# Second attention of a two-block layer: value products that give their output by channels, shares ahead of the transposes, and the output gate by channels

## The reference, cut to what matters

```python
s = jnp.einsum('bhqd,bhkd->bhqk', qblk, kt).astype(jnp.float32) * scale
p = jax.nn.softmax(s, axis=-1).astype(vt.dtype)
return jnp.einsum('bhqk,bhkd->bqhd', p, vt)
...
attn = dense_bidirectional_attention(q, k, v_a)
u_attn = (attn * jax.nn.silu(z_attn)) @ w_attn_out[l]
gates = jax.nn.sigmoid(jnp.concatenate([gate_hy, gate_attn], axis=-1) + b_gate[l])
merged = g_hy * u_hy + g_at * u_attn
x = x + merged @ w_out[l]
```

## Time and profile before

| | |
|---|---|
| median of 3 runs | 801.56 us (801.39 to 801.56) |
| span of the profiled execution | 802.3 us |
| TensorE products busy | 742.8 us, 93% |
| VectorE busy | 465.3 us, 58% |
| ScalarE busy | 321.6 us, 40% |

### The profile page before, as it was taken

How to read it: one execution, slowest core, us unless ns; L and a number is a source line. 1 busy time by engine, 2 the same in 40 slices (tenths; PEclk the granted TensorE clock), 3 DMA queues, 4 the chain that set the end, 5 groups by cost and what they waited for, 6 DMA issues and landing times.

```text
span 802.3 us, 11034 instructions
## 1 busy us (share of the span) xinstructions
PE 742.8 (93%) x4636; PEld 561.2 (70%) x4636; DVE 465.3 (58%) x825; ACT 321.6 (40%) x479; POOL 17.9 (2%) x15
## 2 busy tenths in 40 slices
PE   7999999999999999996799798689999999989998
PEld 7978876888877886553346254247999966668886
DVE  6878965555756666532243221138687798855673
ACT  6464436537437325210111010037665524245631
POOL 0000000000000000000000000001100003000000
PEclk9999999999999999998779999999999999999999
DMA  9855542233439759899999999995563744433311
GB/s 318 246 189 181 168 158 97 102 106 114 149 94 410 282 208 422 323 363 420 420 421 406 420 421 421 418 398 205 164 213 125 233 144 133 157 105 105 105 52 53
DMA packets 63153, 189.97 MB, mean 237 GB/s; under 512 B 7481, under 2 KB 11835, under 8 KB 51132
## 3 DMA queue, kind: packets, MB, share of 16 engines
q1 hardware_dynamic: 61326, 184.44, 62.1%
q10 hardware_dynamic: 1774, 4.79, 1.8%
HBM read 188.16 MB, written 1.05 MB: 236 GB/s over the span
## 4 chain that ended last, share of the span: by engine, by line
PE 60%; DVE 16%; DMA 15%; ACT 6%; issue 1%; POOL 0%; SPq 0%; ACTq 0%; DVEq 0%
PE pb L519 56%; DMA raw<-in_w_exp_up 6%; DVE rawo L1785 4%; PE pb L528 4%; DMA arena<-in_w_exp_gate 3%; DMA WHo<-in_w_exp_up 3%; ACT WH L1282 2%; DMA WHo<-in_w_exp_down 2%; DVE cv_ L1892 1%; ACT arena L1441 1%; DVE arena L2053 1%; DVE arena L1838 1%; DMA c<-in_cst 0%; POOL small L2687 0%; DVE arena L2099 0%
## 5 line engine op out<-in xcount | busy, mean ns | idle before, releaser
L1785 DVE TENSOR_TENSOR rawo<-raw,WH 128x2048 fp32r<-128x2048 f32 (+5 forms) x80 | 172.7, 2176 | 71.2 <-ACT WH L1282 71.1
L519 PE MATMUL pb<-WH,HTh 128*128 128x512 f32 (+2 forms) x384 | 156.2, 407 | 5.9 <-DVE arena L1838 3.1
L1282 ACT ACTIVATE WH<-raw 128x2048 fp32r<-128x2048 f32 (+5 forms) x80 | 144.0, 1823 | 20.6 <-PE pb L519 15.2
L519 PE MATMUL pb<-rawo,HTh 128*128 128x512 f32 (+2 forms) x384 | 148.8, 387 | 0.0
L519 PE MATMUL pb<-WH,HTl 128*128 128x512 f32 (+2 forms) x384 | 148.6, 387 | 0.0
L519 PEld LDWEIGHTS pb<-WH,HTh 128*128 128x128 f32 x384 | 73.1, 190 | 24.9 <-issue 5.3
L519 PEld LDWEIGHTS pb<-rawo,HTh 128*128 128x128 f32 x384 | 72.8, 190 | 14.6
L519 PEld LDWEIGHTS pb<-WH,HTl 128*128 128x128 f32 x384 | 73.1, 190 | 13.3 <-issue 1.0
L519 PE MATMUL pb<-WH,arenao 128*128 128x512 f32 x192 | 59.6, 392 | 1.2 <-DVE arenao L1819 1.2
L519 PE MATMUL pb<-arena 128*32 128x256 f32 (+6 forms) x252 | 58.4, 433 | 1.8 <-ACT arena L1698 0.7
L519 PE MATMUL pb<-raw,arena 128*32 128x256 f32 (+1 forms) x256 | 49.0, 475 | 10.7 <-DMA raw<-in_w_exp_up 6.1
(11 more groups left out here) (363 smaller groups left out, 1270.5 us busy)
## 6 DMA issues: line engine op xcount, KB each, us to landing
raw<-in_w_in SPq DMA_DIRECT2D x46, 1024.0 KB, 5.1
raw<-in_w_exp_up SPq DMA_DIRECT2D x18, 1024.0 KB, 21.3
arena<-in_w_exp_gate SPq DMA_DIRECT2D x13, 1024.0 KB, 22.5
arena<-in_w_exp_down SPq DMA_DIRECT2D x12, 1024.0 KB, 17.0
WHo<-in_w_exp_down SPq DMA_DIRECT2D x9, 1024.0 KB, 23.2
raw<-in_w_out SPq DMA_DIRECT2D x8, 1024.0 KB, 5.8
raw<-in_w_exp_gate SPq DMA_DIRECT2D x8, 1024.0 KB, 15.9
WHo<-in_w_exp_up SPq DMA_DIRECT2D x8, 1024.0 KB, 22.0
```

The source lines that it names most:

```text
L519: return e.matmul(o, l, r, start=start, stop=stop, skip_group_check=True)
L1282: e.activation(h_, r_, ACT.Copy).then_inc(hi.sem, hi.mark(k))
L1785: e.tensor_tensor(l_, r_, h_.bitcast(F32), ALU.subtract).then_inc(lo.sem, lo.mark(k))
```

## The change

1. The value gate `za` is computed with channels on the partitions (`channel_chunk`: per chunk, four blocks of 128 channels, three products of 256 columns each, two blocks in one bank). VectorE drains it, multiplied by the row `RB` that holds each token's norm; then ScalarE takes Silu in one instruction over all 1024 elements of `ZAT`.
2. VectorE takes the reciprocal of a head's sums and scales its exponentials (`shares2`) at the start of the round; the transposes wait for that (`sn2`) and are written ordered by key block, so that a head's 256 queries stand side by side.
3. Value products take the values as the stationary side (64 columns) and the turned shares as 256 moving columns. Two heads share a bank, one on partitions 0 to 63, one on 64 to 127; they are issued once for two heads, in rounds 4, 6, 8 and 10, in bank 4 or 5 in turn.
4. The output comes out by channels, so the transposes of the output go. VectorE multiplies each pair by the gate (`output_gated`), ScalarE makes the upper half (`output_high`) and VectorE the lower (`output_low`), spread over the rounds.
5. `gate 2` goes to banks 4 and 5; `gate 3`, `branch 0` and `branch 1` stay in 6 and 7.
6. The rows of `w_attn_out` are loaded in the order "(c p)" in place of "(p c)"; `OT2` and `RB` are in other places of the SBUF.

```diff
         RD = arena[:, 6144:6400].rearrange("p (t l) -> p t l", t=2)
-        RB = arena[:, 8192:8448]
+        RB = C["matt"][:, 0:256]
         XNs = [x.bitcast(F32) for x in (XNh, XNl)]
...
         UT = tuple(x[:, 0:1024].rearrange("p (c l) -> p c l", c=4) for x in HD_)
-        OT2 = tuple(x[:, 0:4, :] for x in HT)
+        OT2 = tuple(arena_r[:, o:o + 1024].rearrange("p (c l) -> p c l", c=4) for o in (8704, 9728))
         G1 = arena[:, C1:C1 + 2048].rearrange("p (t d) -> p t d", t=2)
...
         G_ = (G1, G2)
-        ZA = rt_[:, 0:1024].rearrange("p (t d) -> p t d", t=2)
-        O2 = rt_[:, 1024:2048].rearrange("p (t d) -> p t d", t=2)
+        ZAT, OG = (rt_[:, o:o + 1024].rearrange("p (c l) -> p c l", c=4) for o in (0, 1024))
         cqj = [sg_[:, 0:384], sg_[:, 384:768]]
...
             weight(("gate", i), w2, 8, 3232 + 512 * i, 512, "(c p)")
-        for key, w, kc, rows_ in (("whn", whn, 4, "(p c)"), ("wa2", wa2, 4, "(p c)"), ("wo2", wo2, 8, "(c p)")):
+        for key, w, kc, rows_ in (("whn", whn, 4, "(p c)"), ("wa2", wa2, 4, "(c p)"), ("wo2", wo2, 8, "(c p)")):
             for i in range(2):
...
         filler("zh", "zh", HT, "ng", ac, True)
-        filler("za", "za", HT, "ng", ac)
+        filler("za", "za", HT, "ng", ve)
         for i in range(4):
...
 
+            def channel_chunk(name, key, c, o, lhs, ready):
+                k, j, last = chunk_at[key][c]
+                lo.wait_ge(e, k)
+                ve.wait_ge(e, (ready, c))
+                w = tuple(x[:, j, :] for x in tile_parts(k))
+                end = c == len(chunk_at[key]) - 1
+                for i in range(4):
+                    ins = mul3(o[i // 2][:, 256 * (i % 2):256 * (i % 2) + 256], tuple(x[:, 128 * i:128 * i + 128] for x in w),
+                               tuple(x[:, c, :] for x in lhs), c == 0 and i % 2 == 0, end)
+                if last:
+                    ins.then_inc(mm.sem, mm.mark(("tile", k), *([(name, 0), (name, 1)] if end else [])))
+
             def fill(n):
...
                         fill_at.rotate(1)
-                    gemm_chunk(name, key, c, open_fill[name], lhs, ready, turned)
+                    if name == "za":
+                        channel_chunk(name, key, c, open_fill[name], lhs, ready)
+                    else:
+                        gemm_chunk(name, key, c, open_fill[name], lhs, ready, turned)
 
...
             fill_at.clear()
-            fill_at.append(6)
-            held_o2 = [ring.take(("o2", t), ve, at=4 + t) for t in range(2)]
+            fill_at.extend((4, 6, 6, 6))
 
...
                 o = ring.take(("p2", h), (ve, ac)[h % 2])
-                ac.wait_ge(e, ("s2", h))
-                for i in range(4):
-                    ins = turn(o[:, i * 128:i * 128 + 128], S2[:, h % 4, i * 128:i * 128 + 128])
+                ve.wait_ge(e, ("sn2", h))
+                for kk in range(2):
+                    for t in range(2):
+                        ins = turn(o[:, kk * 256 + t * 128:kk * 256 + t * 128 + 128],
+                                   S2[:, h % 4, t * 256 + kk * 128:t * 256 + kk * 128 + 128])
                 ins.then_inc(mm.sem, mm.mark(("p2", h)))
 
-            def values2(h):
-                (ve, ac)[h % 2].wait_ge(e, ("p2", h))
+            def values2(p):
+                o = ring.take(("o2", p), ve, at=4 + p % 2)
+                for h in (2 * p, 2 * p + 1):
+                    (ve, ac)[h % 2].wait_ge(e, ("p2", h))
                 ve.wait_ge(e, (("kv", 1), 0))
                 ac.wait_ge(e, (("kv", 1), 1))
-                for t in range(2):
-                    for kk in range(2):
-                        ins = mul(held_o2[t][:, h * 64:h * 64 + 64],
-                                  P2[h % 4][:, t * 256 + kk * 128:t * 256 + kk * 128 + 128],
-                                  V2[:, kk, h * 64:h * 64 + 64], kk == 0, kk == 1)
-                ins.then_inc(mm.sem, mm.mark(("pv2", h)))
+                for kk in range(2):
+                    for i in range(2):
+                        h = 2 * p + i
+                        ins = mul(o[64 * i:64 * i + 64, 0:256], V2[:, kk, h * 64:h * 64 + 64],
+                                  P2[h % 4][:, kk * 256:kk * 256 + 256], kk == 0, kk == 1)
+                ins.then_inc(mm.sem, mm.mark(("pv2", p)))
 
...
                     weights2_T(h - 2)
-                if h >= 3:
-                    values2(h - 3)
-            fill(2)
-            ve.wait_ge(e, "o2")
-            transposed("o2T", lambda t: O2[:, t, :], 4)
+                if h >= 4 and h % 2 == 0:
+                    values2(h // 2 - 2)
             fill(99)
...
                 elif name == "za":
-                    drain(name, ZA, ACT.Silu, by=rg)
+                    ve.wait_ge(e, ("za", 1))
+                    e.activation(ZAT, ZAT, ACT.Silu).then_inc(ac.sem, ac.mark("zas"))
                 elif name[0] == "gate" and i < 2:
...
 
+            def output_high(p):
+                ve.wait_ge(e, ("og", p))
+                e.activation(OT2[0][:, p, :], OG[:, p, :], ACT.Copy).then_inc(ac.sem, ac.mark(("o2h", p)))
+
             for h in range(11):
...
                     fill(1)
+                if h in (5, 7, 9):
+                    output_high((h - 5) // 2)
                 if 2 <= h <= 9 and h % 2:
                     if h >= 6:
-                        mm.wait_ge(e, ("pv2", h - 6))
+                        mm.wait_ge(e, ("pv2", (h - 6) // 2))
                     drain_t(("p2", h - 2), P2[(h - 2) % 4])
-            for i in (2, 3):
-                sigmoid(i)
-            high("o2T", OT2, 4, after=(("gate", 3), 1))
+            sigmoid(2)
+            output_high(3)
+            sigmoid(3)
             fill(99)
...
                                                op0=ALU.mult, op1=ALU.add).then_inc(ve.sem, ve.mark((name, t)))
+                elif name == "za":
+                    for t in range(2):
+                        mm.wait_ge(e, (name, t))
+                        e.tensor_tensor(ZAT[:, 2 * t:2 * t + 2, :], pb((name, t))[:, :].rearrange("p (c l) -> p c l", c=2),
+                                        RB.unsqueeze(1).to_broadcast([128, 2, 256]), ALU.mult).then_inc(
+                            ve.sem, ve.mark((name, t)))
                 elif name[0] == "branch":
...
 
+            def shares2(h):
+                s = h % 4
+                ac.wait_ge(e, ("s2", h))
+                e.reciprocal(rsum[:, :, h:h + 1], ssum[:, :, h:h + 1]).then_inc(ve.sem, ve.mark(("rs2", h)))
+                ve.wait_ge(e, ("rs2", h))
+                for t in range(2):
+                    cut = S2[:, s, t * 256:t * 256 + 256]
+                    ins = e.tensor_scalar(cut, cut, rsum[:, t, h:h + 1], None, ALU.mult)
+                ins.then_inc(ve.sem, ve.mark(("sn2", h)))
+
+            def output_gated(p):
+                mm.wait_ge(e, ("pv2", p))
+                ac.wait_ge(e, "zas")
+                e.tensor_tensor(OG[:, p, :], pb(("o2", p))[:, 0:256], ZAT[:, p, :], ALU.mult).then_inc(
+                    ve.sem, ve.mark(("og", p), ("o2", p)))
+
+            def output_low(p):
+                ac.wait_ge(e, ("o2h", p))
+                e.tensor_tensor(OT2[1][:, p, :], OG[:, p, :], OT2[0][:, p, :].bitcast(F32), ALU.subtract).then_inc(
+                    ve.sem, ve.mark(("o2T", p)))
+
             for h in range(11):
+                if 2 <= h <= 9:
+                    shares2(h - 2)
+                if h in (5, 7, 9):
+                    output_gated((h - 5) // 2)
                 fill(1, h < 10)
...
                     fill(1)
+                if h in (6, 8, 10):
+                    output_low((h - 6) // 2)
                 if 2 <= h <= 9 and h % 2 == 0:
                     if h >= 6:
-                        mm.wait_ge(e, ("pv2", h - 6))
+                        mm.wait_ge(e, ("pv2", (h - 6) // 2))
                     drain_t(("p2", h - 2), P2[(h - 2) % 4])
-            ac.wait_ge(e, ("s2", 7))
-            for t in range(2):
-                rs = rsum[:, t, 0:8]
-                e.reciprocal(rs, ssum[:, t, 0:8]).then_inc(ve.sem, ve.mark(("rs2", t)))
-                mm.wait_ge(e, ("pv2", 7))
-                ve.wait_ge(e, ("rs2", t))
-                e.tensor_tensor(hd(O2[:, t, :]), hd(pb(("o2", t))[:, :]), rs.unsqueeze(2).to_broadcast([128, 8, 64]),
-                                ALU.mult).then_inc(ve.sem, ve.mark(("o2", t)))
-                ac.wait_ge(e, ("za", t))
-                ve.wait_ge(e, ("o2", t))
-                e.tensor_tensor(O2[:, t, :], O2[:, t, :], ZA[:, t, :], ALU.mult).then_inc(ve.sem, own("o2"))
+            output_gated(3)
             weights(used(("whn", 0)))
-            low("o2T", OT2, 4)
+            output_low(3)
             fill(99)
```

## The result

The changed kernel takes 807.41 us (median of 7 runs, 803.79 to 808.92), the kernel before 801.56 in the same session. The ratio is 1.0052, with a 95% interval of 1.0036 to 1.0068: slower by 2.9 to 5.5 us, 4.2 in the middle. The medians stand further apart, 5.85 us, since three of the seven runs lie at 803.8 to 804.8 and four at 807.4 to 808.9; I go by the ratio. A second session gave 1.0041 (1.0022 to 1.006). Predicted were +2.5 us and a slower kernel.

The account below looks back on a forecast made before the run. TensorE, busy 93% of the span, was taken as the bound. Shift and start +1.9, first half of the head loop +2.1, second half -1.5 gave +2.5 on 801.56: 804.1 us, range 799.2 to 806.0.

Parts of the forecast that it names:

- the likeliest case: Whole kernel: +2.5 us, 804.1 us, with its own range 802.6 to 805; chance 0.41.
- the forecast's own signs of being wrong: First stall under 1.5 us, full clock behind it, or head loop not within 1.5 us of 51.8.
- Part 1, the value gate: Before the second transform: VectorE's drain and ScalarE's Silu delay the next split, shifting all by 3.5 us; TensorE stands 2.9.
- The clock: Behind the new 2.9 us stall before the second transform: the granted clock falls, costing 1.6 us.
- Part 2, the banks: Before the first scores: the 3.14 us stall at gate 2 goes, a 1.5 us wait for head 0's copies comes.
- Part 3, the value products: Head loop: a pair's 8 records take 0.95 us, four pairs 3.8 instead of 6.7, so 2.9 us gained.
- rival 3: Value products in the head loop: column halves don't run together, +0.8 us per pair; +4.2, 805.8 us; chance 0.07.
- Part 5, the shares: Head loop: 0.8 us per head on VectorE, and TensorE's transposes wait, 2.4 us for head 2.
- Rival 4: Transposes of head 2: shares never hold them, the 2.4 us stall vanishes; -2.7, 798.9 us; chance 0.18.
- The second half: Head loop's later part, with gate 3's tiles: 2.2 us more standing against -2.2 and -1.5, coming to -1.5 us.
- The step that failed: Stall before the first scores: 1.5 us with no clock price, since a 1.47 us stall at 698.86 had none.
- Rival 2: Head loop: the clock falls after the 2.4 us stall as well, up to 1.85 more; +3.9, 805.5 us; chance 0.12.

Follow-up runs that it names:

- the second profile: The profile of the changed kernel run once more with no edit, in the third session: ratio 1.0041 to the kernel before.
- the drain alone: The kernel before, with only the value gate drained by VectorE and ScalarE's Silu following: ratio 1.0054, median 806.24 us.
- the Silu behind the upper half: The changed kernel, with ScalarE's upper half of the next weight tile ahead of the value gate's Silu: ratio 0.9996 to the kernel before.
- the products in the stall: The changed kernel with twelve more products on TensorE in its stall before the second transform: ratio 1.003 to the kernel before.
- that experiment: The changed kernel with gate 2 back in banks 6 and 7: ratio 1.0093 to the kernel before.
- three further moves at once: The changed kernel with value gate and shares reordered, plus head 0's copies, maximum and exponentials moved ahead of splits: ratio 0.9982 to the kernel before.

## Why the prediction was right, and where it was off

The direction was right, and so was the mechanism but for one step; the sum was 1.3 us short in the profile (3.84 against 2.5). By the ratio the kernel stands at 805.7, above the likeliest case's own range (802.6 to 805) and just inside the wide one (to 806.0). One of the forecast's own signs of being wrong came: the head loop was to be within 1.5 us of 51.8, and it took 53.74, or 54.25 in the second profile.

- **Part 1, the value gate:** shift 3.52 against 3.5, the stall 2.93 against 2.9. Shown by the drain alone, which brings the cost to the kernel before (+0.54%), and by the Silu behind the upper half, which takes it away (3.6 to 4.5 us under the changed kernel's two ratios).
- **The clock:** 1.5 us against 1.6, by the products in the stall. But it is a chance and not a rule: of the six profiles with a stall of 2.9 us or more ahead of T2, it fell behind that stall in three. So it is in part luck that the first scores came at +1.90 in the profile at hand; without the fall they come at +0.4, where the forecast had +0.3.
- **Part 2, the banks:** the first scores at +1.90 against +1.9, behind a stall of 1.69 against 1.5. With the old banks they come at 69.97, with the new ones and no fall behind T2 in either at 66.84: 3.1 gained, and spent on the later gate, as the prediction had it. At P 1.75 of it was left (see that experiment).
- **Part 3, the value products:** the 8 records take 1.01 us on the chain against 0.95, and rival 3 is out. But the records aren't all that a pair costs. From a head's transposes to the next ones TensorE's timeline has 1.54 us with a pair between (744.69 to 746.23) and 0.43 without (740.17 to 740.60), and the dense product after them starts 0.04 later. A pair thus adds 1.15 us, and the four save 2.1 us of the 6.7, not 2.9. The drains of the Trainium skill's rule that changing the mode drains the engine (page "TensorEngine Tiling (Array Packing)", section "Tiling Modes") have at most 0.29 us a pair to hide in: 1.15 less four times 0.215, the distance at which the pairs of records start. How much of that the drains are no run shows; the sum had put nothing for them.

```profile
740.17 0.60 PE L527 MATMUL pb<-c,XN 128*128 128x128 f32 x4
740.60 0.60 PE L527 MATMUL pb<-c,arena 128*96 128x128 f32 x4
...
744.69 0.60 PE L527 MATMUL pb<-c,XN 128*128 128x128 f32 x4
745.22 1.08 PE L518 MATMUL pb<-cv_,arena 128*64 128x256 f32 x8
746.23 0.64 PE L527 MATMUL pb<-c,arena 128*96 128x128 f32 x4
```

The row of the chain:

```profile
735.10 1.01 PE pb L518 x8
```

- **Part 5, the shares:** the stalls are 2.17 for head 2 (2.4), none for head 1 (0.5; it is 0.30 in the second profile, where no fall followed the first scores), 1.11 at the branch (1.4), 0.87 for head 6 (1.0), none for head 7 (0.1). The steps themselves cost 0.8 as taken. Rival 4 failed: the shares did hold the transposes. The reason given for the stall at the branch, the shares of head 5 ahead of the gate's drain, failed: it stands at 1.11 without any shares. That TensorE, with fewer value products, is simply early for the same drain is argued and not shown. The second half came to -1.36 against -1.5, and there two errors offset each other: three pairs cost 3.45 us and not 2.85, and TensorE's stalls grew by 1.5 us and not by 2.2.
- **The step that failed:** "A stall of 1.47 us, at 698.86, had no such price", after which the sum put no price of the clock on the stall of 1.5 us before the first scores. That stall measured 1.69 and a fall followed it: the first half of the loop, from the first scores to the transposes at 736.04 (730.27 before), took 3.3 us more where 2.1 were summed. The missing 1.2 are in the main products at half speed: from the first to the second scores it is 5.74 us here and 4.14 without a fall. In the kernel with the Silu behind the upper half, where no fall came, the first half took 2.2 us more than before, the second as much as here, and the loop 52.66 against 52.4 predicted. Rival 2 had the kind of loss (a second fall, +3.9) and put it behind the stall of head 2, where the changed kernel's second profile has it.

What stays open: why the 1.68 us stall is followed by a fall in six of eight profiles and the stall of 1.45 to 1.50 us before the convolution's transposes in none of fourteen. They differ in length by 0.2 us and in the work on either side, and no run changed one alone.

## What to carry to other kernels

Where each engine works through a queue in order, price a moved step by what stands behind it: the drain cost 1.3 us on VectorE, and put TensorE's next transform 3.5 us later because a split on another engine stood behind the step that followed it. Put the step that feeds the bottleneck ahead of the splitting, and the step that nobody waits for behind it; the same work then was 5 us faster instead of 4 slower. Move one at a time: a stall before a point may be slack for a wait behind it, and three further moves at once lost most of the gain.

## What the runs showed of the hardware

- **The program alone doesn't set the granted clock.** The same kernel fell behind different stalls in two profiles, and stalls of 2.92 or 2.93 us with the same products before and after were followed by a fall in two profiles and by none in three. A fall cost 1.5 us in the transform (8.63 against 7.13) and 1.6 behind the first scores (5.74 against 4.14), of which 1.1 was left at the end of the loop (53.74 against 52.66). So a stall can carry, besides its length, a price that comes in some executions only, and one profile of each kernel can mislead by more than a microsecond.
- **Column halves overlap whatever the order of issue.** Four products of 256 columns on two halves took 1.01 to 1.09 us at the full clock, one half at a time in the program or alternating; at 0.215 per record one after the other they would be 1.7. Between full-array work such a group adds 1.15 us to TensorE's queue.
